# Mixture-of-experts blocks: two experts to a block of 64 slots, and output rows scattered to their token's place

## What is computed

```python
def route(h, w_router, e_bias):
    scores = jax.nn.sigmoid((h @ w_router).astype(jnp.float32))
    biased = scores + e_bias.astype(jnp.float32)
    ...
    _, idx = lax.top_k(jnp.where(emask, biased, -jnp.inf), TOP_K)
    w = jnp.take_along_axis(scores, idx, axis=1)
    return idx, w / jnp.sum(w, -1, keepdims=True) * ROUTED_SCALE

# every expert e, on the rows that chose it:
hid = jax.nn.silu(xb @ w1[e]) * (xb @ w3[e])     # 1024 -> 256, twice
y   = (hid @ w2[e]) * wt[:, None]                # 256 -> 1024
```

## Time and profile before

| what | value |
|---|---|
| median of 3 runs | 1441.91 us (1437.85 to 1443.77) |
| span of the profiled execution | 1441.5 us |
| TensorE busy | 1142.5 us, 79% |
| DVE, ACT, GpSimd busy | 467.1, 249.1, 174.2 us |
| HBM read and written | 335.37 and 46.37 MB |
| mean granted clock of TensorE | 0.925 |

### The profile page before, as it was taken

How to read it: one execution, slowest core, us unless ns; L and a number is a source line. 1 busy time by engine, 2 the same in 40 slices (tenths; PEclk the granted TensorE clock), 3 DMA queues, 4 the chain that set the end, 5 groups by cost and what they waited for, 6 DMA issues and landing times. The chain is left out here.

```text
span 1441.5 us, 23491 instructions
## 1 busy us (share of the span) xinstructions
PE 1142.5 (79%) x7919; PEld 741.4 (51%) x7920; DVE 467.1 (32%) x873; ACT 249.1 (17%) x502; POOL 174.2 (12%) x284
## 2 busy tenths in 40 slices
PE   3299999996685799586888887999867698778763
PEld 2197787784564344343555544555544454444421
DVE  4324323337843114774222221222211121111246
ACT  1122212325454000101111111111111011011000
POOL 0001211100000000002120111101110110110055
PEclk9999999996789799787999999999999899898987
DMA  8575786438363861193469899998799999999774
GB/s 290 122 269 193 252 272 216 156 132 295 111 201 108 299 189 69 57 415 103 153 199 376 332 345 387 376 391 294 267 368 372 371 381 379 384 382 380 321 257 151
DMA packets 120488, 382.58 MB, mean 265 GB/s; under 512 B 14501, under 2 KB 31845, under 8 KB 95726
## 3 DMA queue, kind: packets, MB, share of 16 engines
q1 hardware_dynamic: 105742, 338.12, 64.9%
q0 software_dynamic: 12960, 40.53, 9.1%
q10 hardware_dynamic: 1728, 3.15, 0.6%
HBM read 335.37 MB, written 46.37 MB: 265 GB/s over the span
## 5 line engine op out<-in xcount | busy, mean ns | idle before, releaser
L1561 PE MATMUL PS<-W,XT 128*64 128x256 f32 x2048 | 263.0, 413 | 85.5 <-DMA W<-w 83.0
L1561 PEld LDWEIGHTS PS<-W,XT 128*64 128x64 f32 x2048 | 179.6, 149 | 191.9 <-issue 137.9
L1610 PE MATMUL PS<-W,hidT 128*64 128x512 f32 x512 | 124.0, 605 | 2.8 <-DVE hidT L1679 2.0
L1679 DVE COPY hidT<-PS 128x128 f32<-128x128 f32 x64 | 18.7, 292 | 311.6 <-PE PS L1602 310.8
L425 DVE TENSOR_TENSOR w_lo<-raw,w_hi 128x2048 fp32r<-128x2048 f32 x26 | 59.5, 2289 | 148.4 <-ACT w_hi L387 148.4
L1632 ACT ACTIVATE sg<-PS 64x256 f32<-64x256 f32 x64 | 24.2, 378 | 445.3 <-PE PS L1561 445.3
L358 PE MATMUL PS<-w_hi,u_hi 128*128 128x512 f32 x240 | 95.6, 398 | 0.0
L358 PE MATMUL PS<-w_hi,u_lo 128*128 128x512 f32 x240 | 94.8, 395 | 0.0
L358 PE MATMUL PS<-w_lo,u_hi 128*128 128x512 f32 x240 | 94.7, 395 | 0.0
L1575 PE MATMUL PS<-W,XTo 128*64 128x256 f32 x736 | 84.5, 381 | 7.3 <-DVE Yo L1673 6.7
L1575 PEld LDWEIGHTS PS<-W,XTo 128*64 128x64 f32 x736 | 60.4, 137 | 39.8 <-issue 25.5
(11 more groups left out here) (314 smaller groups left out, 1470.6 us busy)
## 6 DMA issues: line engine op xcount, KB each, us to landing
W<-w SPq DMA_DIRECT2D x192, 1024.0 KB, 12.5
raw<-w_in SPq DMA_DIRECT2D x26, 1024.0 KB, 9.1
expert_rows<-Y SPq DMA_DIRECT2D x128, 128.0 KB, 9.1
oaT<-w_ada SPq DMA_DIRECT2D x8, 1536.0 KB, 7.7
expert_rows<-zeros SPq DMA_DIRECT2D x23, 512.0 KB, 6.7
expert_rows<-Yo SPq DMA_DIRECT2D x46, 128.0 KB, 2.9
obT<-w_ada SPq DMA_DIRECT2D x8, 512.0 KB, 8.1
kc<-cache_k_diff SPq DMA_DIRECT2D x8, 512.0 KB, 4.6
```

Of the source, the lines that this page charges most:

```text
L1561: mm = pe.matmul(PS[64 * h:64 * h + 64, 2 + i % 2, 0:F], XT[:, i % 2, k], t.W13[:, i, h, k], start=k == 0, stop=k == KD - 1)
L1610: mm = pe.matmul(PS[64 * h:64 * h + 64, 5 + i % 2], hidT[:, i % 2, j], t.W2[:, i, j, CW * h:CW * h + CW], start=j == 0, stop=j == 1)
```

## The change

Blocks of 64 slots now hold 32 slots each of two experts 2n and 2n + 1 (`BASE` = 32, `PAIRS` = 32 blocks); an expert's tokens beyond 32 go to extra blocks of 64, as before. `up` and `down` of a pair work on 32 columns for each expert, four column tiles in turn. The four weight slots are two pairs (`PW` = 2), and a pair's `up` waits for both. Each row is scattered by GpSimd to its token's place in the tensor, half a row (2 KB) per index, from a table `t.dest` that `routing` makes beside `t.tokens`; an empty slot has an index beyond the bound in `t.dest`, and is not stored, and token 0 in `t.tokens`, and gathers row 0. So no fill of zeros is needed, and `combine` reads plain strided rows with SyncE into 24 buffers of their own. `XG` and `XGo` lie in the memory of `hT`, and `XG` has two buffers instead of four. The extra block has PSUM banks of its own for its up and its down projection.

```diff
-XB = (TOK * TOPK - 1) // SLOTS
-NBLK = E + XB
+BASE = 32
+PAIRS = E // 2
+XB = E + (TOK * TOPK - E * (BASE + 1)) // SLOTS
+NBLK = PAIRS + XB
...
-WB = 4
+PW = 2
+WB = 2 * PW
...
 # attention_prompt, sync
-            for n in fills:
...
 # routing, vector
-            link(dve.tensor_scalar(ext[:, :], cnt[:, :], float(SLOTS), None, ALU.is_gt))
+            link(dve.tensor_scalar(ext[:, :], cnt[:, :], float(BASE), None, ALU.is_gt))
...
-                link(dve.tensor_tensor(SL[:, n % 2], io[:, 0:SLOTS].unsqueeze(1).to_broadcast([P, TOPK, SLOTS]),
-                                       sf[:, :].unsqueeze(2).to_broadcast([P, TOPK, SLOTS]), ALU.is_equal))
+                dve.tensor_tensor(SL[:, :, :], io_m[:, :].unsqueeze(1).to_broadcast([P, TOPK, P]),
+                                  sf[:, :].unsqueeze(2).to_broadcast([P, TOPK, P]), ALU.is_equal)
...
-                dve.tensor_scalar(CB[:, n % 2], CBf[:, :, :], tk[:, n:n + 1], None, ALU.mult).then_inc(code_done, 1)
+                dve.tensor_tensor(CB[:, :, :], CB[:, :, :], at[:, n].unsqueeze(2).to_broadcast([P, TOPK, NBLK]), ALU.mult).then_inc(code_done, 1)
             dve.wait_ge(list_mm, NT)
+            link(dve.tensor_scalar(none[:, :], lists, 0.5, float(2 ** 16), ALU.is_lt, ALU.mult))
+            link(dve.scalar_tensor_tensor(place[:, :], lists, -1.0, none[:, :], ALU.add, ALU.add))
+            link(dve.tensor_scalar(dest[:, :], lists, -1.0, 0.0, ALU.add, ALU.max))
+            link(dve.tensor_scalar(t.tokens[:, 0:NBLK], dest[0:SLOTS, :], 3, None, ALU.logical_shift_right))
...
+            dve.tensor_scalar(t.dest[:, :], place[:, :], 2.0, half[:, 0:1], ALU.mult, ALU.add)
...
 # experts, sync
-                if not last:
-                    load_expert(sp, t, at(it, i, WB), i)
+            def body(n, i, it, fixed):
+                sp.wait_ge(yy_ev, n + 1)
+                for c in range(2):
+                    used = sp.value_load(t.ov[0:1, bass.ds(n * 2 + (c + 1), 1)], min_val=0, max_val=XB)
+                    sp.wait_ge(o_ye, used + 1)
+                    stand_alone(sp)
+                    if within(fixed, PW):
+                        load_expert(sp, t, n * 2 + (c + WB), 2 * i + c)
...
 # experts, gpsimd
+            def step(g):
                 pool.wait_ge(o_xt, g + 1)
+                gather_extra(g + 1, g + 2)
+                pool.wait_ge(o_ye, g + 2)
+                pool.tensor_copy(dxo[:, 0:1], t.dest[:, bass.ds(g + PAIRS, 1)]).then_inc(o_dx, 1)
+                pool.wait_ge(o_dx, g + 1)
...
+                pool.indirect_dma_start(t.y_dram, bass.IndirectOffsetOnAxis(ap=dxo[:, 0:1], axis=0), Yo[:, :], None,
+                                        bounds_check=TOK * TOPK * 2 - 1, oob_is_err=False).then_inc(o_out, 16)
+            def body(n, i, it, fixed):
+                if within(fixed, 3):
+                    pool.wait_ge(xt_mm, n + 2)
+                    gather(n + 3, (i + 1) % 2, n + 4)
+                pool.wait_ge(yy_ev, n + 1)
...
+                pool.indirect_dma_start(t.y_dram, bass.IndirectOffsetOnAxis(ap=dx[:, i:i + 1], axis=0), Y[:, i], None,
+                                        bounds_check=TOK * TOPK * 2 - 1, oob_is_err=False).then_inc(y_out[i], 16)
+                for c in range(2):
+                    extra(pool, n * 2 + c, step)
...
 # experts, tensor
             def up(n, i, it):
-                pe.wait_ge(t.wexp_in[i], (it + 1) * 48)
+                for c in range(2):
+                    pe.wait_ge(t.wexp_in[2 * i + c], (it + 1) * 48)
...
                     for h in range(2):
-                        mm = pe.matmul(PS[64 * h:64 * h + 64, 2 + i % 2, 0:F], XT[:, i % 2, k], t.W13[:, i, h, k], start=k == 0, stop=k == KD - 1)
+                        for c in range(2):
+                            mm = pe.matmul(PS[64 * h + 32 * c:64 * h + 32 * c + 32, UP_B + i, 0:F], XT[:, i, k, 32 * c:32 * c + 32],
+                                           t.W13[:, 2 * i + c, h, k], start=k == 0, stop=k == KD - 1)
...
 # the extra block: up may start before Yo of the block before is evicted
-                    pe.wait_ge(o_ye, g + 1)
...
+            def body(n, i, it, fixed):
+                if within(fixed, 1):
+                    up(n + 1, nxt[1], nxt[0])
                 pe.wait_ge(hid_done, n + 1)
...
 # combine
-        G = sb("G", [P, TOPK, D])
+        G = sb("G", [P, NT, TOPK, D])
...
-                    pool.indirect_dma_start(G[:, k], None, t.y_dram, bass.IndirectOffsetOnAxis(ap=t.rows[:, n, k:k + 1], axis=0)).then_inc(row_in[k], 16)
...
+            for n in range(NT):
+                for k in (3, 0, 4, 1, 5, 2, 6, 7):
+                    sp.dma_start(G[:, n, k], rows[P * n:P * n + P, k]).then_inc(row_in[n][k], 16)
```

More of the change, by code:

```diff
@@ L1320, in _ @@
                 for k in range(TOPK):
-                    mm = pe.matmul(PS[0:SLOTS, 5, 0:NBLK], SL[:, n % 2, k], CB[:, n % 2, k], start=n + k == 0, stop=n == NT - 1 and k == TOPK - 1)
+                    mm = pe.matmul(PS[:, 5, 0:NBLK], SL[:, k], CB[:, k],
+                                   start=n + k == 0, stop=n == NT - 1 and k == TOPK - 1)
                 mm.then_inc(list_mm, 1)
@@ L1411, in _ @@
                 dve.wait_ge(rank_mm, n + 1)
[L1412 to L1415, removed]
+                link(dve.tensor_tensor(code2[:, :], PS[:, n, 64:64 + E], io_b[:, :], ALU.add))
@@ L1416, in _ @@
+                link(dve.scalar_tensor_tensor(code[:, :], PS[:, n, 64:64 + E], float(BASE), base[:, :], ALU.is_ge, ALU.mult))
+                link(dve.tensor_tensor(code[:, :], code[:, :], code2[:, :], ALU.add))
                 link(dve.tensor_tensor(tmp[:, :, :], oh[:, n], code[:, :].unsqueeze(1).to_broadcast([P, TOPK, E]), ALU.mult))
                 link(dve.tensor_reduce(ck[:, :], tmp[:, :, :], AX.X, ALU.add))
-                link(dve.tensor_copy(t.rows[:, n], ck[:, :]))
-                link(dve.tensor_scalar(si[:, :], t.rows[:, n], SLOTS - 1, None, ALU.bitwise_and))
@@ L1452, in experts @@
[L1452 to L1457 removed]
+        XG = t.hT[:, :, :].rearrange("p k q -> p (k q)")[0:SLOTS, 0:2 * D].rearrange("p (i d) -> p i d", i=2)
@@ L1480, in stand_alone @@
             eng.sem_inc(waited, 1)
+        LOOPS = (PAIRS - 3) // PW
         def loops(eng, body):
-            for i in range(WB):
-                body(0, i, False)
-            with eng.Fori(1, E // WB - 1) as it:
-                for i in range(WB):
-                    body(it, i, False)
-            for i in range(WB):
-                body(E // WB - 1, i, True)
+            for n in range(PW):
+                body(n, n, 0, n)
+            with eng.Fori(1, LOOPS) as it:
+                for i in range(PW):
+                    body(it * PW + i, i, it, None)
+            for n in range(LOOPS * PW, PAIRS):
+                body(n, n % PW, n // PW, n)
@@ L1492, in _, with within @@
+        def within(n, ahead):
+            return n is None or n + ahead < PAIRS
         @block.sync
         def _(sp):
-            def store_extra(g):
-                sp.wait_ge(o_ye, g + 2)
-                for h in range(2):
-                    sp.dma_start(t.y_dram[bass.ds((g + E) * SLOTS, SLOTS), CW * h:CW * h + CW], Yo[64 * h:64 * h + 64, :]).then_inc(o_out, 16)
-            def body(it, i, last):
-                sp.wait_ge(yy_ev, at(it, i, 1))
-                for h in range(2):
-                    sp.dma_start(t.y_dram[bass.ds(at(it, i) * SLOTS, SLOTS), CW * h:CW * h + CW], Y[64 * h:64 * h + 64, i % 2]).then_inc(y_out[i % 2], 16)
-                extra(sp, at(it, i), store_extra)
-                if not last:
-                    load_expert(sp, t, at(it, i, WB), i)
@@ L1530, in _ @@
-            for i in range(WB):
-                gather(i, i, i + 1)
-            pool.tensor_copy(ixo[:, 0:1], t.tokens[:, E:E + 1]).then_inc(o_ix, 1)
-            pool.wait_ge(o_ix, 1)
-            pool.indirect_dma_start(XGo[:, :], None, t.h_dram, bass.IndirectOffsetOnAxis(ap=ixo[:, 0:1], axis=0)).then_inc(o_in, 16)
-            def body(it, i, last):
-                extra(pool, at(it, i), gather_next)
-                if not last:
-                    pool.wait_ge(xt_mm, at(it, i, 1))
-                    gather(at(it, i, WB), i, at(it, i, WB + 1))
@@ new lines, in _ @@
+            gather(0, 0, 1)
+            gather(1, 1, 2)
+            gather_extra(0, 1)
+            pool.dma_start(Yo[:, 0:128], t.h_dram[0:P, 0:128]).then_inc(o_out, 16)
+            pool.wait_ge(xt_mm, 1)
+            gather(2, 0, 3)
+            loops(pool, body)
+            for i in range(PW):
+                pool.wait_ge(y_out[i], 16 * PAIRS // PW)
+            total = pool.value_load(t.ov[0:1, E:E + 1], min_val=0, max_val=XB)
+            pool.wait_ge(o_out, total * 16 + 16)
+            stand_alone(pool)
```

234 lines of the change are left out of this document (112 added, 122 removed).

## The result

The changed kernel takes 2131.58 us (median of 4 runs, 2126.94 to 2132.29) where the kernel before takes 1442.84: a ratio of 1.477, 95% interval 1.474 to 1.480. It is 48% slower. The forecast was 2040, the range 1780 to 2220.

A forecast was written before the change was run, and what follows sets the result against it. It took the stream of expert weights to bound the kernel. From 695 us, periods 900, extra blocks 204 and 150, and an end of 3, 24 and 5 gave 1981; with combine 2040 us, range 1780 to 2220.

The forecast's parts named there:

- Rival 1: Expert stage: same serial ring, but the extra blocks' gather is early and the clock holds, 1690 to 1780 us; chance 0.11.
- Rival 3: Expert stage: loads keep ahead after all and TensorE becomes the bound, 1480 us; chance 0.04.
- Rival 4: Expert stage: faster, loads queued as now and gathers hidden, 232 MB moved instead of 247, 1405 us; chance 0.05.
- Rival 2: TensorE's up and down projections: the column tiles don't run side by side, +167 us, 2205 us; chance 0.05.
- Period: Expert stage, one pair without extra blocks: release, loads, gather and scatter, computation and clock in series, 30.0 us, 30 times.
- Extra blocks of odd experts (c = 1): Expert stage: 20 blocks partly overlapping the other slot's load; ten pairs lose 6.4 us, three 18.4, one 30.4: 150 us.
- 15.5 beside a load: Cost in us of one extra block while weights are loading, its gather landing in 7.6 us on full queues.
- Extra blocks of even experts (c = 0): Expert stage: each delays both loads of a pair, 17 blocks at 12 us, 204 us.
- The end: End of expert stage: last pair without an up projection 3 us, its two extra blocks 24, last scatter's landing 5.
- First Y: Start of expert stage: first output evicted at 695 us instead of 688.7, by the longer routing.
- Routing's 6 us: Routing on DVE: larger tables, f32 list product, tail operations and counting add 6 us (4 to 10).
- Combine: After the expert stage: plain loads by SyncE instead of GpSimd's 24 gathers save 6 us (12 to 0).

The follow-up runs named there:

- experiment 1: Changed kernel with the down projection and extra blocks of a pair done before the next pair's up projection: 1711.7 us, ratio 1.186.
- experiment 4: Kernel before, blocks of 64 and direct stores kept, with experts loaded two at a time in a ring of pairs: 1839.4 us, ratio 1.274.
- experiment 2: Changed kernel with GpSimd gathering two extra blocks ahead, as soon as XGo is free: 1871.3 us, ratio 1.296.
- experiment 6: Kernel before, with GpSimd gathering the next extra block only after the eviction of the block before: 1585.3 us, ratio 1.099.
- experiment 3: Changed kernel with both the down projection first and the early gather for extra blocks: 1437.7 us, ratio 0.995.
- experiment 5: Changed kernel's scatter, routing and combine with single-expert blocks of 64, the old ring of four and the early gather: 1445.5 us, ratio 1.002.
- experiment 7: Changed kernel with 46 unread matmuls ahead of the up projection of eight pairs, pairs from 14 on written out: 2111.6 us, ratio 1.465.

## Why the prediction was right, and by how much it was off

It is slower, as forecast, and the span lies inside the range. The mechanism held: the ring frees its slots behind the consumer that waits (experiments 1 and 4), and the gather stands behind the scatter (experiments 2 and 6). Of the rivals none came. Rival 1 needed the gather early and the clock high; a gather was issued 4.1 us behind the down projection even on idle queues, and the clock stood at 0.50 behind the waits. Rival 3, TensorE as the bound at 1480 us, asked for slots free before `up(n+1)`: experiment 1 made just that, with the late gather kept, and took 1711.7. Rival 4 asked for hidden gathers besides, which is experiment 3: 1437.7 for its 1405. It counted 15 MB fewer as 37 us; experiment 5 wrote 12.3 MB less and gained nothing. Rival 2 is refuted by the 64 records in 3.66 us: the forecast had 3.8 for a pair on four tiles.

The span is 89 us above the forecast. By its terms:

- *Period.* 30.5 for 30.0, times 30: +15. Two errors inside it cancel. The load part, with gather and scatter beside it, is 20.1 us from the first issue to the up projection, where the sum had 17.5 + 1.5, 1.1 less; the clock costs 2.2 (5.83 less 3.66, and the same by the periods of experiment 7), where it had 2.9. Release (1.0) and computation without the clock (9.4 - 2.2 = 7.2 for 7.1) were right.
- *Extra blocks of odd experts (c = 1).* This is the term that was mis-sized. One costs 10.3 us beyond the period for 6.4 (40.6 to 41.1), two 24.3 for 18.4, three 37.2 for 30.4. With the mixed pairs that makes some 64 us. The step that failed is "15.5 beside a load": such a block takes 19.4 to 20.2 where it is the first of its pair, and 17.9 to 18.7 behind one of the even expert. In the second timeline of an extra block above, the gather is issued 5.9 us after the down projection's end (1648.89 to 1654.76) for 3.9 in the working; before the index copy GpSimd spent 1.8 us on nothing that shows ("1.80 <-issue"), where its code loads registers and branches. All seven pairs whose even expert has no extra block show 1.5 to 1.9 us there, the others 0.2 to 0.4. The landing took 8.4 for 7.6, and the down projection at the low clock 3.56 for 1.94.
- *Extra blocks of even experts (c = 0).* 12.5 for 12, times 17: +9. The working had 1 us for the low clock in an idle block; the gather came when it should (4.1 us after the down projection, landed in 3.7), and the down projection alone lost 1.7.
- *The end.* The last pair 6.7 for 3, its two extra blocks 27 for 24: +7. Last landing 5.3 for 5.
- *First Y.* 690.5 for 695: -4.5. Routing's 6 us were nearly right: from the router's first matmul to the first Y evicted it is 85.8 us (604.65 to 690.45) for 80.9 (607.75 to 688.67), +4.9. But that matmul comes 3.1 us earlier, for which the sum had nothing. It is not the zero fills: prompt attention takes 70.4 us on TensorE in both. The kernel of experiment 4, which has the fills, reaches the router at 603.53, so this much varies from execution to execution.
- *Combine.* 58.7 for 58.3: the 6 us of gain came, with SyncE's plain loads.

15 + 64 + 9 + 7 - 4.5 = 90.5, where 89 were measured.

The Trainium skill, page "TensorE: Matmul & The Clock Gate", section "HAM oscillation — how this bites in real kernels", has each tile of a kernel start cold after its wait; the 5.83 and 3.66 us of experiment 7 agree with the rule, but the loss was 2.2 us, less than half of the up projection's time, since the clock rose under way. The Trainium skill, page "DMA: Bandwidth & Descriptors", section "Anatomy of one DMA — SWDGE (gpsimd) path", gives a transfer from GpSimd about 2.0 us and its bytes at 436 GB/s, an estimate of 2.6 us for 64 rows of 4 KB. The rows say 3.7 on idle queues and 8.4 beside a load, and by the page's figure the extra blocks would have been forecast lower still.

The prediction gave the empty slots no price. Their 22 us were in the landings that it took from the earlier trace rows, where empty slots gather row 0 as well. And it called the stream the bound of the kernel before; by experiment 6 that kernel's extra blocks were a bound beside it. This touched no term of the sum, since in the changed kernel nothing hides them either.

## What to carry to other kernels

Count the slots that are free while the consumer waits, not the slots: four slots as two pairs, with the next pair's first use ahead of the current pair's last, prefetch nothing, and cost 395 us in a kernel where nothing else was touched. Do the work that frees a buffer before the work that waits for the next one, on every engine, and on an in-order queue put an early request ahead of the wait for a late result. With both faults mended, the whole change, with TensorE's work on base blocks halved, was worth half a percent: the stream of weights had been busy 0.93 of the stage, and packing brought 15 more extra blocks. Read that share, and count those blocks, first.

## What was not expected of the hardware

- Bytes on GpSimd's software queue took more of the engines' time than those on the hardware queue: 0.30 against 0.37 to 0.38 MB per percent of 100 us (experiment 5). Scatters that saved 12.3 MB saved no time; that the one is the reason for the other is argued, not shown.
- Where a pair's even expert had no extra block, GpSimd needed 1.5 to 1.9 us between the base block's scatter and the index copy of the odd expert's extra block, with nothing in the profile but "issue"; elsewhere 0.2 to 0.4.
- Behind a wait of 4 to 5 us in the chain of an extra block the down projection took 3.68 us, in the changed kernel (granted clock 0.50, 1.2 GHz) and in experiment 6, against 1.94 behind the early gather in nearly all blocks of experiment 2.
- Skipped rows of a gather cost less than fetched ones: 6 MB fewer were 22 us where the gather was in the chain, and 9 in the version of experiment 3.
